# Attention in a two-block layer kernel: weighing the probabilities by a product with a diagonal matrix that also turns them

## What is computed

```python
s = jnp.where(mask, jnp.einsum('td,sd->ts', q, k) * scale - slope * dist, NEG)
p = jax.nn.softmax(s, axis=-1)
o = gt[0] * o_cmp + gt[1] * (p_sel @ v_sel) + gt[2] * (p_win @ v_win)
```

## Time and profile before

| | us |
|---|---|
| median of 3 runs | 3935.03 |
| lowest and highest | 3928.12, 3937.2 |
| the profiled execution, its own time | 3939.57 |
| its span from first to last instruction | 3937.6 |
| attention phase, first score to last output, in its trace | 958.8 to 1329.3 |

### The profile page before, as it was taken

The page is one execution under the profiler, slowest core; times in us unless marked ns, Lnnn a source line. Parts: engine busy times, 40 slices in busy tenths (PEclk is TensorE's granted clock), DMA queues, the critical chain, the costliest instruction groups (busy, mean ns, idle before and its releaser), DMA issues. The chain is left out here.

```text
span 3937.6 us, 55743 instructions
## 1 busy us (share of the span) xinstructions
PE 3528.7 (90%) x23201; PEld 2909.9 (74%) x23201; DVE 1777.3 (45%) x2725; ACT 869.4 (22%) x1258; POOL 1030.7 (26%) x491
## 2 busy tenths in 40 slices
PE   5999899987999888999999889878983989999997
PEld 4878777776777776888888767667872768888886
DVE  4752555422777644555555636043433322323233
ACT  2112121121343202111111220144322031111112
POOL 3332222333111233121212044122212341212121
PEclk9999999998999998999999989989886989999998
DMA  3353333333000212322222045300002121111111
GB/s 96 134 173 114 108 97 108 97 112 105 8 8 1 97 54 79 114 75 85 75 85 75 23 155 148 104 18 19 19 3 80 40 70 40 61 38 59 37 48 43
DMA packets 309558, 285.53 MB, mean 73 GB/s; under 512 B 21326, under 2 KB 276864, under 8 KB 308408
## 3 DMA queue, kind: packets, MB, share of 16 engines
q1 hardware_dynamic: 283882, 209.82, 18.0%
q10 hardware_dynamic: 25186, 72.62, 5.0%
q0 software_dynamic: 288, 0.20, 0.1%
HBM read 221.64 MB, written 60.95 MB: 72 GB/s over the span
## 5 line engine op out<-in xcount | busy, mean ns | idle before, releaser
L708 POOL TENSOR_TENSOR ffn_wlo<-ffn_raw,ffn_whi 128x1024 fp32r<-128x1024 f32 x88 | 211.4, 2404 | 1067.4 <-ACT ffn_whi L896 1011.7
L203 PE MATMUL up<-h_hi,ffn_whi 128*128 128x512 f32 x1408 | 439.5, 394 | 20.3 <-POOL h_lo L402 20.3
L203 PE MATMUL up<-h_lo,ffn_whi 128*128 128x512 f32 x1408 | 436.3, 391 | 0.0
L203 PE MATMUL up<-h_hi,ffn_wlo 128*128 128x512 f32 x1408 | 435.5, 391 | 0.0
L192 POOL TENSOR_TENSOR whi<-raw,ones 128x1024 fp32r<-128x1024 f32 (+1 forms) x87 | 160.5, 1845 | 851.7 <-PE acc L1404 492.8
L203 PEld LDWEIGHTS up<-h_hi,ffn_whi 128*128 128x128 f32 x1408 | 263.3, 189 | 78.3 <-POOL h_lo L402 14.0
L203 PEld LDWEIGHTS up<-h_lo,ffn_whi 128*128 128x128 f32 x1408 | 265.9, 189 | 56.2
L203 PEld LDWEIGHTS up<-h_hi,ffn_wlo 128*128 128x128 f32 x1408 | 265.7, 189 | 56.1
L1404 PE MATMUL acc<-h_hi,whi 128*128 128x512 f32 x816 | 275.7, 420 | 8.9 <-POOL h_lo L402 8.8
L799 DVE TENSOR_TENSOR ffn_prod<-ffn_act,up 128x1024 f32<-128x1024 f32 x44 | 53.7, 1221 | 464.5 <-PE up L203 464.5
L1404 PE MATMUL acc<-h_lo,whi 128*128 128x512 f32 x816 | 259.3, 400 | 0.0
(11 more groups left out here) (542 smaller groups left out, 6625.8 us busy)
## 6 DMA issues: line engine op xcount, KB each, us to landing
raw<-w_in SPq DMA_DIRECT2D x51, 512.0 KB
projT<-proj_stage ACTq DMA_DIRECT2D x51, 512.0 KB, 2.7
ffn_ada_raw<-w_ada SPq DMA_DIRECT2D x24, 1024.0 KB, 5.0
ffn_raw<-w_up SPq DMA_DIRECT2D x44, 512.0 KB
ffn_draw<-w_down SPq DMA_DIRECT2D x11, 1024.0 KB, 6.9
ffn_raw<-ffn_w_gate SPq DMA_DIRECT2D x22, 512.0 KB
ffn_raw<-ffn_w_up SPq DMA_DIRECT2D x22, 512.0 KB
ffn_draw<-ffn_w_down SPq DMA_DIRECT2D x11, 1024.0 KB, 4.8
```

Source lines behind the costliest of these rows:

```text
L203: last = nc.tensor.matmul(acc[:, t, :], w[:, k, w_cols], x[:, k, t * HALF:(t + 1) * HALF], start=(k == 0 and i == 0), stop=(k == k_tiles - ...
L708: nc.gpsimd.tensor_tensor(w_lo[i][:], raw[i][:], w_hi[i][:], ALU.subtract).then_inc(s[f"up_split{i}"], 1)
```

## The change

The transposition and the scaling become one product. For P the tile of exp values and D the diagonal matrix of the 128 numbers, the product of the stationary P with the moving D is the turned P with each column scaled. VectorE no longer scales `att_prob`; it writes the 128x128 matrix D, as the identity times the number of each row, into a new buffer `att_diag` (one for each r). In TensorE's program an f32 matmul with `att_diag` as moving operand stands where the transposition with `ident` stood. The semaphores, their values, the groups, the banks and the order on every engine are as before, and each engine has as many instructions in its program as before. Both new buffers lie in free SBUF.

```diff
+    diag = [mem.at(f"att_diag{r}", (206.375, 205)[r], [P, P]) for r in range(2)]
...
                     for t in range(nt):
-                        last = nc.tensor.transpose(ps[f"pt{n % 2}"][:, t * P:(t + 1) * P], prob[r][:, (t0 + t) * P:(t0 + t + 1) * P], ident[:])
+                        last = nc.tensor.matmul(ps[f"pt{n % 2}"][:, t * P:(t + 1) * P], prob[r][:, (t0 + t) * P:(t0 + t + 1) * P], diag[r][:],
+                                                start=True, stop=True)
                     last.then_inc(s[f"grouped{n % 2}"], 1)
...
-                n = tiles(i, r) * P
                 dve.wait_ge(s[f"weighted{r}"], j // 2 + 1)
-                nc.vector.tensor_scalar(prob[r][:, 0:n], prob[r][:, 0:n], small[r][:, 3:4], None, ALU.mult).then_inc(s[f"scaled{r}"], 1)
+                nc.vector.tensor_scalar(diag[r][:], ident[:], small[r][:, 3:4], None, ALU.mult).then_inc(s[f"scaled{r}"], 1)
```

## The result

The changed kernel takes 3951.36 us (median of 6 runs, 3949.02 to 3958.59) where the kernel before takes 3936.11 (6 runs, 3928.12 to 3939.37). The ratio is 1.0044 with an interval of 1.0031 to 1.0058: slower by 0.44%, some 17 us. The forecast was 3963 with a range of 3943 to 3990, of which 3955 to 3978 was the band of the forecast itself; the first rival ("the clock no longer falls") named 3953.

What follows compares the result with a forecast made beforehand. TensorE was taken as closest to the bound, VectorE second. 57.0 us of added products less 16.8 and 12 hidden left 28 us on 3939.6, or 3963 as a median; range 3943 to 3990.

Steps and rivals of the forecast that it cites:

- the first rival: At starts of heads: the clock no longer falls, giving back 10 us, so 3953; chance 0.20.
- 528 products for transpositions: On TensorE: a product is two records, a transposition one; 0.108 us for each additional record, 57.0 us more.
- hidden by the waits of narrow jobs: From a head's start into its query tile 4: waits hide 2.1 of 2.6 us a head, 16.8 us.
- hidden at the starts of heads: Six head starts with GpSimd at work: TensorE's waits and VectorE's shorter scaling hide 2.0 us each, 12 us.
- wide jobs: Query tiles 4 to 7: TensorE alone sets the pace; no cover for its additional work, VectorE's saving worth nothing.
- The rival with four distances: At the products: each takes four times a transposition's 0.108 us, 171 us more, about 4077; chance 0.03.
- The other side: The diagonal is cheap, VectorE was the bound: at 0.05 us a product fits into the waits, 3920; chance 0.05.

Runs made afterwards that it cites:

- the pair without GpSimd: Without GpSimd's query preparation (and loads) for heads 2 to 7: kernel before, ratio 0.9929, phase 336.9 us; changed kernel, ratio 1.0033, phase 386.6 us.
- the product alone: Kernel before with an f32 product with the identity in place of the transposition, VectorE scaling the whole width as before: ratio 1.0046, phase 386.8 us.
- the diagonal alone: Kernel before with VectorE writing the 128-column diagonal instead of scaling, TensorE transposing as before, weights left out: ratio 0.9916, phase 333.6 us.
- the kernel with delayed scores: Kernel before with five idle TensorE products ahead of the last window job's scores in heads 0 to 5: ratio 0.9953, phase 349.2 us.
- the kernel with the product in fp32r: Changed kernel with att_prob and att_diag of type fp32r, so a product is one record: ratio 0.9918, 3904.44 us.

## Why the prediction was right where it was, and where it wasn't

The direction and the range were right, the size was too large by a factor of 1.7: 28 us forecast, 16.1 us in the phase and 17 by the ratio. The sum against what the runs showed:

| term | forecast | measured | from |
|---|---|---|---|
| 528 products for transpositions | +57.0 | +63.4 | wide jobs, where nothing hides it: 0.120 a tile |
| hidden by the waits of narrow jobs | -16.8 | -13.7 | 63.4 less 386.6 - 336.9, the pair without GpSimd |
| hidden at the starts of heads | -12 | -33.6 | 370.5 - 336.9, and 386.6 both with and without GpSimd |
| sum | +28 | +16.1 | |

**The price of a product** was a little too low. Two records for a product and one for a transposition, as the earlier trace rows said, is what the trace after shows. But the sum took one more record at an unchanged distance, 0.108 us, and the exchange costs 0.120 us a tile. It can be read from the seventh head, where the loads wait for no other engine and GpSimd doesn't work. From the turning of its query tile 4 (window) to that of its query tile 7 (window) there are 36 tiles, before:

```profile
1266.15 0.73 PE L2138 MATMUL pt<-ident,att_prob 128*128 128x128 f32 x5
...
1284.28 0.73 PE L2138 MATMUL pt<-ident,att_prob 128*128 128x128 f32 x5
```

and after:

```profile
1269.83 1.33 PE L2139 MATMUL pt<-att_diag,att_prob 128*128 128x128 f32 x10
...
1292.27 1.33 PE L2139 MATMUL pt<-att_diag,att_prob 128*128 128x128 f32 x10
```

That is 18.13 us before and 22.44 us after, 4.31 us more. In these traces most transpositions start 0.109 us after the one before, most records of a product 0.112 us, and the first two records of a product's group are often 0.16 us apart; so the second record and the somewhat wider distances together make the 0.120. The last head, for which 5 us had been forecast, gets longer by 6.0 us. The rival with four distances is refuted, and so is the factor of four in the Trainium skill's page "TensorE: Matmul & The Clock Gate" (Terms), as a price at this shape: the rows show about two.

**The waits of narrow jobs** were sized nearly right. That they cover TensorE's work and that the loop of VectorE doesn't wait for it holds, since none of them is left. The eight steps of TensorE take 17.96 us in the trace of before (1201.20 to 1219.16, by the first transposition of each) and 18.87 us in that of the changed kernel (1203.88 to 1222.75). So 24 tiles add 0.91 us of their 2.88, and 2.0 us are hidden, where I had 2.1. Only in the first head, whose narrow jobs begin at the lower clock, is nothing won in sum: in the pair without GpSimd it gets longer by 7.9 us, the full price of its 66 tiles. Seven heads give 13.7 us.

**The starts of heads** is the step that failed. I let GpSimd's start be a fixed anchor, with VectorE held behind it at the same instructions, so that only 13 tiles of TensorE's work could go into the waits. And I called VectorE's saving in wide jobs worth nothing, as TensorE doesn't wait for it there. Both miss that GpSimd's start is itself set by TensorE, through the last scores of the head. When TensorE gets slower in the wide jobs, or VectorE faster, VectorE begins the 1024-wide job ahead of GpSimd's start, and the instruction that TensorE needs soonest is no longer held. In the trace of before it missed this by little. GpSimd began at 1232.03, and the 128x1 product ahead of the scaling, which takes 0.16 us when it isn't held, began 0.44 us behind:

```profile
1232.47 1.47 DVE L2216 TENSOR_TENSOR att_small<-att_small,nsa_gates 128x1 f32<-128x1 f32 x1
```

Unheld, the scaling would have begun some 0.6 us behind GpSimd's start; at the first of the six starts it missed by 0.1 us only (998.89 against 998.78).

Experiments show it from both sides: VectorE faster in wide jobs (31.5 us gained), TensorE slower just ahead of that start (21.3 us gained, with useless work). In the changed kernel the slower TensorE is enough by itself: the product alone has the same phase, so the shorter scaling is worth nothing there.

**The first rival** came about, clock and time (3953 against 3951.36), though partly for another reason: I gave it 10 us for the clock and left waits of 1.2 and 0.5 us in place. The waits vanished altogether. The clock's own share is 7.5 us where only the waits are filled. That 3953 came so near is luck in part: the starts of heads hid 11.6 us more than the 22 which this rival had for them, and against that the products cost 6.4 us more and the narrow jobs hid 3.1 us less. The same errors, offsetting each other in part, kept the measured time within the range of the forecast. I had held against this rival that a wait of over 1 us remained, and that was the wrong step's consequence.

By the rule of the Trainium skill's page "TensorE: Matmul & The Clock Gate" (Part 4), that transposes don't count as activity for the clock gate, the clock should fall while transpositions take a good part of TensorE's time. The diagonal alone and the kernel with delayed scores have transpositions throughout and a granted clock of 1.00 at all six starts of heads; what they don't have is TensorE standing for 1.8 and 1.5 us. No run here shows the rule at work. Whether a transposition counts for less than a product is not tested: the waits were filled with products.

**The other side** asked for a record at 0.055 us or less and was refuted by its own condition. But there was something in it that I hadn't seen: shorter work of VectorE, though TensorE never waits for it in wide jobs, is worth 36.9 us by itself. The product beside it takes 53.0 us (386.6 against 333.6), so the two together lose.

## What to carry to other kernels

An f32 product in place of an f32 transposition costs a second record for each tile, here 0.120 us; when the operands may be rounded to fp32r it doesn't, and then weighing by a diagonal matrix was a gain here, of 0.8%. Most of that gain comes from the order of VectorE and GpSimd: 31.5 of the 36.9 us with the diagonal alone came from wide jobs, where TensorE never waited for VectorE. Don't judge the saving on an engine by who waits for it in the stretch where it falls: ask which later event it runs against, above all the start of an engine whose work holds it up, when that start is tied to a third engine. And read the price of an exchange from whole steps where nothing hides it, before and after, rather than from the distance of single records.

## What of the hardware was not expected

While GpSimd works, a VectorE product of 128x1 elements takes 1.4 to 2.3 us instead of 0.16, and a scaling 1.8 to 2.7, whether it has 128 columns or 1024. Not every instruction is held: in the same stretch of before a reciprocal takes 0.16 us (at 1238.24) and a copy out of PSUM 0.28 us (at 1237.21). It goes the other way too: in the kernel with the product alone two instructions of GpSimd take 4.34 us instead of 3.85, when the 1024-wide scaling of 0.75 us is begun first.

```profile
1239.67 4.34 POOL L2100 TENSOR_TENSOR att_q_high<-att_q,ones 64x1024 fp32r<-64x1024 f32 x2 [38.36 <-PE sc L2128]
```

A load of 128 columns takes 0.14 us for a transposition and 0.19 us for a product, and yet the distance from record to record is about the same (0.109 and 0.112 us). The loads by source line, ns min/median/max, before and after:

```profile
L2138 PEld LDWEIGHTS pt<-ident,att_prob x528: 137/140/230, 964.7 to 1325.0; 128*128 128x128 f32 x176
```

```profile
L2139 PEld LDWEIGHTS pt<-att_diag,att_prob x1056: 186/192/338, 963.1 to 1339.6; 128*128 128x128 f32 x176
```

In the kernel with the product in fp32r the clock stayed at half its level in the first head while TensorE was busy without a gap; with the diagonal alone it had come up at about 972 us.

```profile
972.00:980.00 8.00, 8.00 (x31) 6.62 (x31) 5.09 (x17) 2.61 (x7) 0.00 (x0) 0.50 0.00 0
...
990.00:998.00 8.00, 8.00 (x56) 7.13 (x55) 4.82 (x14) 3.50 (x7) 0.00 (x0) 0.93 0.01 2
```

It is one profiled execution, and why the clock came up some 18 us later is left open; nothing was tried on it.
